# Sample blocks at alternate heads, a DMA rate of 280 in the list schedule, and later weights for the second head

## The chip, the cores and the metric

The kernel runs on 8 cores of one Trainium2 chip. Every core runs the same program on its own data; nothing is exchanged between cores. The metric is the device time of the slowest core in microseconds. A profile is one execution, read on the slowest of its cores (core 5 here). Names of the engines in profile rows: PE is TensorE (PEld its weight loads), DVE is VectorE, ACT is ScalarE, POOL is GpSimd, SP is SyncE, which only issues DMAs here.

## The reference

One inference step of a two-layer decoder, for 8 prompts of 2048 tokens and 128 samples of 4 new tokens, model width 1024. A core takes one prompt and 16 samples (64 sample tokens).

- Layer 0, HGRN2, 16 heads of 128 channels: `proj = x @ w_in` gives q, forget logit, value and gate for each head. With `f = lb + (1 - lb) * sigmoid(z)` the state is `S_t = diag(f_t) S_{t-1} + (1 - f_t) v_t^T` and the output `o_t = S_t^T q_t`; then a per-head RMS norm, times `silu(gate)`, `@ w_out`. A prompt starts from a zero state, a sample from its given state; both return their final states.
- Layer 1, chunked gMLP, chunks of 128 positions, 16 groups of 128 channels: u and v through gelu, v layer-normalised, `mixed = tril(W_s) v + b_s` in each group and chunk, `out = u * mixed * silu(z)`, `@ w_out`. The normalised v rows of the samples are an output.
- After each layer `x = LayerNorm(ALPHA * x + mixer(x))`.

## The kernel before, in words

**Tiling and stages.** A core works through its prompt in two passes of 1024 tokens (`sbi` 0 and 1), as 8 tiles of 128 tokens, or 2 blocks of 512 (`bi`). The 64 sample tokens are a ninth tile (`XTS`). A pass has these stages: transposed x in `XT`; layer 0's 16 heads, `for h in range(H)`, each with two prompt blocks (`l0_prompt`) and, for eight of the heads, one sample block (`l0_sample`); the output projection with layer norm (`outproj_ln`); layer 1's first eight groups of u and z (`uz`), the v tiles with the spatial gating (`v_tile`), the last eight groups of u and z, and the second output projection. Each head's sample block is computed once in the whole kernel, as its weights pass by: before, heads 0 to 7 in the first pass and heads 8 to 15 in the second (`if h // 8 == sbi`). The sample tile goes through the later stages in the second pass alone.

**A prompt block** (`l0_front`, `l0_prompt`, `l0_out`). TensorE makes four projections of the block (24 matmuls of 512 columns and 32 of 128 for the values). ScalarE makes tanh, two silu, a logarithm (L617) that needs the gate constants `lbc`, two exponentials, copies, and the norm's logarithm and exponential; functions of different tables need a table load between them. VectorE scans the logarithms (L640, L642), GpSimd scales the chunk states (L686) and multiplies by the gate (L706). A sample block does the same for 64 tokens, and in addition loads 2 x 512 KB of states on the SP queue, converts them to bf16 on ScalarE, multiplies values by a mask on VectorE (L731), adds into the states and stores 2 x 512 KB. Its state buffers `S0` exist twice, picked by `k = h % 2`.

**Weights.** The projection weights of head h lie in two of four `WH` buffers. `wia_load(h + 2)` stands behind head h: its two DMAs, issued by GpSimd, wait until head h's projections have read the buffers. They convert float32 to bf16 (512 KB land for 1 MB read). `wbig_load` brings an eighth of an output or v weight; in both passes the heads 1 to 8 each load one eighth of `woa`. At head 2 of the first pass the spatial weights are loaded too (`WST`, `WSM`, `GB`), at head 4 they are masked, 32 GpSimd products.

**Start.** `x_first(j)` loads an x tile as float32 into one of four staging buffers `XSF` (the same memory as `S0`), transposes it on TensorE, and copies it to `XT[j]` with ScalarE and VectorE. Before: tile 0, weights of head 0, tiles 1 to 3, sample tile, weights of head 1, tiles 4 to 7. The constants `lbc` come by two small DMAs of the SP queue (L533 and before) and some steps on VectorE and ScalarE (L534 to L540).

**The order of work.** No engine's order is written out by hand. The code records every operation with a cost and its dependences (`Plan.rec`, `Plan.dma`). `Plan.schedule` then plays the program through once: at each step it picks, among the ready operations of all engines, the one that can start first, and by priority where starts are within 0.05 us. The priority is the place in the program, less `early`, less the length of the chain behind the operation. The result is one fixed order for each engine. `Plan.emit` writes it out with semaphore waits. An engine does its list strictly in order; if an operation is late on the chip, all behind it on that engine wait. A DMA is an operation of the queue that issues it, and its landing is planned thus, with one pipe for all DMAs of the core:

```python
            if o.dma:
                dmafree = max(s + o.cost, dmafree) + o.nbytes / self.DMABW
                o.fin = dmafree + self.DMALAT
```

Before, `DMABW` is 200.0e3 bytes per us and `DMALAT` 2.0 us. `nbytes` is 1 << 20 for a weight DMA and 1 << 19 for a state DMA. The plan does not re-order anything on the chip, and it does not know what the chip really does.

Of the kernel before, what the change touches and what calls it, by code (L numbers as in the profile page):

```python
# [11 lines left out]
ALU = mybir.AluOpType  # L12
# [76 lines left out]
class Plan:  # L89
# [11 lines left out]
    DMABW = 200.0e3  # L101
# [227 lines left out]
def build_nc():  # L329
# [25 lines left out]
    lng = din("lng", [2, 1, 1024])  # L355
    lnb = din("lnb", [2, 1, 1024])
# [6 lines left out]
    with ExitStack() as es:  # L363
        S = Plan(nc, es)
# [50 lines left out]
        LNG = sb("LNG", [128, 1024], F32)  # L415
        LNB = sb("LNB", [128, 1024], F32)
# [85 lines left out]
        XSF = [S0[0][0], S0[0][1], S0[1][0], S0[1][1]]  # L502
# [40 lines left out]
        def lnload(l):  # L543
            S.dma("sp", LNG[:], lng[l, 0, :].partition_broadcast(128), LNG, True, 524288)
            S.dma("sp", LNB[:], lnb[l, 0, :].partition_broadcast(128), LNB, True, 524288)
# [35 lines left out]
        def wia_load(h):  # L581
            for hf in range(2):
                w = WH[(h % 2) * 2 + hf]
                S.dma("pool", w[:].rearrange("p (a b) -> p a b", b=512), wia[h, :, hf * 2048:(hf + 1) * 2048].rearrange("p (a b) -> p a b", b=512),
                      w, True, 1 << 20, early=300)
# [122 lines left out]
        def l0_sample(h):  # L708
            N = 64
            k = h % 2  # L710
# [114 lines left out]
        def v_tile(ti):  # L825
# [15 lines left out]
            for nb in range(4):  # L841
                V(lambda v, nb=nb: v.tensor_scalar(out=vg[nb][0:rows, :], in0=vg[nb][0:rows, :], scalar1=st[0:rows, 24:25], scalar2=st[0:rows, 26:27],  # L842
                                                   op0=ALU.subtract, op1=ALU.mult), (vg[nb], st), (vg[nb],), 0.4, port=True)
                P(lambda e, nb=nb: e.tensor_tensor(out=ng[nb][0:rows, :], in0=vg[nb][0:rows, :], in1=GB[0:rows, nb * 512:(nb + 1) * 512], op=ALU.mult),  # L844
                  (vg[nb], GB), (ng[nb],), 1.05)
# [37 lines left out]
        for sbi in range(2):  # L883
            if sbi == 0:
                x_first(0, 0, XSF[0])
                wia_load(0)
                for j in range(1, 4):
                    x_first(j, j * 128, XSF[j])
                x_first(8, 0, XSF[0])
                wia_load(1)  # L890
                for j in range(4, 8):
                    x_first(j, j * 128, XSF[(j + 1) % 4])
            else:
                lnload(0)
# [4 lines left out]
            for h in range(H):  # L899
# [8 lines left out]
                if h // 8 == sbi:  # L908
                    l0_sample(h)
# [22 lines left out]
                if sbi == 0 and h == 4:  # L932
# [24 lines left out]
                    lnload(0)  # L957
# [91 lines left out]
```

How the kernel before makes its waits and increments, by code:

```python
    def emit(self):  # L249
# [16 lines left out]
                key, val, sem, sval = tok[d]  # L266
                if kn.get(key, 0) >= val:
                    continue
                waits.append((sem, sval))
                for k, v in clock[d].items():
                    if kn.get(k, 0) < v:
                        kn[k] = v
            eng = self.eng[o.e]
            embed = not o.dma and o.e != "pe"
            for sem, sval in (waits[:-1] if embed else waits):
                eng.wait_ge(sem, sval)
            ins = None
            for n_, fn in enumerate(o.fns):
                ins = fn(eng)
                if n_ == 0 and embed and waits:
                    ins.wait_op(waits[-1][0], waits[-1][1], "sem-ge")
            if o.dma:
                b = o.sbuf
                if b.sem is None:
                    b.sem = self.newsem("d")
                b.cnt += 16
                ins.then_inc(b.sem, 16)
                tok[i] = (b, b.cnt, b.sem, b.cnt)
                if o.is_out:
                    outs.append(tok[i])
# [5 lines left out]
                sem = esem[o.e][-1]  # L296
                ins.then_inc(sem, 1)
                tok[i] = (o.e, q + 1, sem, q % self.EPOCH + 1)
            c = dict(kn)
            c[tok[i][0]] = tok[i][1]
            clock[i] = c
        fin = {}
        for key, val, sem, sval in outs:
            fin[key] = max(fin.get(key, (0, None)), (sval, sem), key=lambda t: t[0])
        for sval, sem in fin.values():
            self.eng["sp"].wait_ge(sem, sval)
```

## Time and profile before

| | before |
|---|---|
| median of 3 runs | 1448.02 us (1445.81 to 1459.31) |
| the profiled execution's own time | 1448.55 us |
| its span on core 5 | 1447.5 us |
| spans of the 8 cores | 1419.9 to 1447.5 us |
| TensorE busy | 1313.5 us (91%) |
| ScalarE busy | 918.5 us (63%) |
| VectorE busy | 901.2 us (62%) |
| GpSimd busy | 577.2 us (40%) |
| mean granted TensorE clock, core 5 | 0.959 |
| x tile load (ARENA<-xp), median from issue to landing | 3.5 us |

How to read it: the span runs from the first to the last instruction; the execution's own time has about 1 us around it. Busy shares are means over stages with different limits, so they do not say what a stage waits for. The first pass's heads run from about 22 to 430 us, the second's from about 745 to 1103 us; the rest are output projections and the gMLP layer.

### The profile page before, as it was taken

To read this page: it belongs to the slowest core of one execution; us is meant where nothing else is said; L and a number is where in the kernel's file an instruction comes from. 1 tells how busy PE (TensorE), PEld (TensorE's weight loads), DVE (VectorE), ACT (ScalarE), POOL (GpSimd) and SP (SyncE) were. 2 spreads that over 40 slices of the span, in tenths; PEclk is the share of its full clock that TensorE was granted. 3 is DMA by queue.
4 is the path that set the end of the run, shared out by engine and by line. 5 is a ranking of instruction groups with operands and counts; after the bars stand their busy time and mean duration, and the time that the engine had idled before them with its cause. 6 is when DMAs were issued, how large, how long until landed. Compare 5 with 4: busy or idle time off the path is not lost.

```text
span 1447.5 us, 25232 instructions; the slowest of 8 cores (1419.9 to 1447.5 us)
## 1 busy us (share of the span) xinstructions
PE 1313.5 (91%) x9592; PEld 710.2 (49%) x9592; DVE 901.2 (62%) x1932; ACT 918.5 (63%) x1543; POOL 577.2 (40%) x700
## 2 busy tenths in 40 slices
PE   6898887889979989997999999998988998999997
PEld 3555454545534434443455655555554443444443
DVE  1688775546757434752676666767786733476467
ACT  1899898879952434642149999999993244465310
POOL 3257554423330416563003444545463051677400
PEclk9999888889989999998999999999999999999999
DMA  8488585433322863097234556465544195319211
GB/s 197 124 151 156 129 160 104 92 55 59 60 59 73 108 97 59 11 159 121 74 102 90 92 92 93 91 148 150 119 122 126 58 130 88 60 30 132 44 54 70
DMA packets 61254, 142.58 MB, mean 98 GB/s; under 512 B 5584, under 2 KB 32208, under 8 KB 61136
## 3 DMA queue, kind: packets, MB, share of 16 engines
q0 software_dynamic: 41072, 78.80, 36.9%
q1 hardware_dynamic: 20064, 62.16, 13.9%
q8 instruction: 79, 1.29, 0.4%
q14 instruction: 39, 0.32, 0.1%
HBM read 192.73 MB, written 27.00 MB: 152 GB/s over the span
## 4 chain that ended last, share of the span: by engine, by line
PE 44%; ACT 31%; DVE 9%; DMA 9%; POOL 4%; issue 3%; SPq 0%; DVEq 0%; ACTq 0%; POOLq 0%
PE PS L326 43%; DMA WBIG<-wv 6%; ACT L617 3%; ACT ARENA L617 3%; ACT L612 3%; DMA WH<-wuz 2%; ACT PS L646 2%; DVE ARENA L640 2%; POOL ARENA L844 2%; ACT ARENA L612 2%; ACT ARENA L614 2%; ACT ARENA L702 2%; ACT ARENA L616 1%; ACT PS L650 1%; ACT ARENA L656 1%
## 5 line engine op out<-in xcount | busy, mean ns | idle before, releaser
L326 PE MATMUL PS<-XT,WH 128*128 128x512 bf16 x2560 | 600.3, 389 | 15.4 <-DMA WH<-wuz 10.5
L326 PEld LDWEIGHTS PS<-XT,WH 128*128 128x128 bf16 x2560 | 247.1, 100 | 306.9 <-issue 49.5
L326 PE MATMUL PS<-WBIG,OT 128*128 128x512 bf16 x1024 | 228.5, 383 | 4.0 <-POOL OT L706 3.3
L326 PEld LDWEIGHTS PS<-WBIG,OT 128*128 128x128 bf16 x1024 | 99.8, 99 | 123.5 <-issue 9.5
L326 PE MATMUL PS<-WBIG,XT 128*128 128x512 bf16 x512 | 119.5, 389 | 9.8 <-DMA WBIG<-wv 9.8
L326 PE MATMUL PS<-WH,XT 128*128 128x128 bf16 x2048 | 126.9, 221 | 0.7 <-DVE SCO L666 0.7
L326 PE MATMUL PS<-ARENA 128*128 128x128 bf16 (+4 forms) x1360 | 114.7, 214 | 12.3 <-DVE ARENA L651 3.8
L326 PEld LDWEIGHTS PS<-WH,XT 128*128 128x128 bf16 x2048 | 118.7, 99 | 6.1 <-issue 2.1
L706 POOL TENSOR_TENSOR OT<-ARENA 128x512 bf16<-128x512 f32 x64 | 81.2, 1270 | 96.8 <-DVE ARENA L704 96.8
L770 DVE BATCH_NORM_STATS2 ARENA<-ARENA 128x6 f32<-128x512 f32 (+1 forms) x136 | 93.8, 690 | 41.6 <-ACT ARENA L838 38.5
L813 DVE SCALAR_TENSOR_TENSOR ARENA<-ARENA,PS 128x512 f32<-128x512 f32 (+1 forms) x80 | 46.4, 592 | 108.7 <-ACT ARENA L812 108.7
L644 POOL TENSOR_TENSOR ARENA<-ARENA 128x5 f32<-128x5 f32 x64 | 17.6, 275 | 214.9 <-DVE ARENA L642 214.7
L640 DVE TENSOR_TENSOR_SCAN ARENA<-scm,ARENA 128x64 f32<-128x64 f32 x256 | 65.1, 314 | 58.1 <-ACT ARENA L617 57.6
L326 PEld LDWEIGHTS PS<-ARENA 128*128 128x128 bf16 (+2 forms) x1360 | 76.5, 103 | 42.6 <-issue 28.1
L844 POOL TENSOR_TENSOR ARENA<-ARENA,GB 128x512 bf16<-128x512 f32 (+1 forms) x68 | 83.2, 1245 | 32.6 <-DVE ARENA L842 32.4
L811 ACT ACTIVATE ARENA<-PS 128x512 f32<-128x512 f32 (+1 forms) x80 | 41.8, 523 | 85.6 <-PE PS L326 84.9
L773 ACT ACTIVATE ARENA<-ARENA,lbc 128x1 f32<-128x1 f32 (+1 forms) x51 | 15.0, 296 | 112.9 <-DVE ARENA L772 109.3
L326 PEld LDWEIGHTS PS<-WBIG,XT 128*128 128x128 bf16 x512 | 49.0, 100 | 73.9 <-issue 22.0
L686 POOL TENSOR_TENSOR ARENA<-ARENA 128x384 bf16<-128x384 f32 x64 | 61.4, 959 | 59.8 <-DVE ARENA L683 59.0
L812 ACT ACTIVATE ARENA<-PS 128x512 f32<-128x512 f32 (+1 forms) x80 | 41.8, 524 | 64.0 <-PE PS L326 63.9
L838 ACT ACTIVATE ARENA<-PS 128x512 f32<-128x512 f32 (+1 forms) x68 | 39.4, 597 | 65.4 <-PE PS L326 60.1
L625 DVE CAST ARENA<-PS 128x512 bf16<-128x512 f32 (+1 forms) x80 | 48.0, 602 | 44.7 <-PE PS L326 44.3
(162 smaller groups left out, 2250.2 us busy)
## 6 DMA issues: line engine op xcount, KB each, us to landing
WH<-wia POOLq DMA_DIRECT2D x64, 512.0 KB, 8.6
ARENA<-s SPq DMA_DIRECT2D x32, 512.0 KB, 5.9
sso<-ARENA SPq DMA_DIRECT2D x32, 512.0 KB, 4.3
WH<-wuz POOLq DMA_DIRECT2D x32, 512.0 KB, 9.0
ARENA<-xp SPq DMA_DIRECT2D x24, 512.0 KB, 3.5
WBIG<-woa POOLq DMA_DIRECT2D x16, 512.0 KB, 8.0
WBIG<-wv POOLq DMA_DIRECT2D x16, 512.0 KB, 26.4
WBIG<-wob POOLq DMA_DIRECT2D x16, 512.0 KB, 15.9
```

Of the source, the lines that this page charges most:

```text
L326: return lambda t: t.matmul(out(), lhsT=lhsT, rhs=rhs, start=start, stop=stop, skip_group_check=True)
L612: A(lambda a, b=b: a.activation(out=tz[:, 0:N], in_=b.v(N), func=AF.Tanh, scale=-0.5), (b,), (tz,), c_act(N), "tanh")
L617: A(lambda a: a.activation(out=lf[:, 0:N], in_=tz[:, 0:N], func=AF.Ln, scale=nc1, bias=c0), (tz, lbc), (lf,), c_act(N) + 0.2, "ln")
L625: V(lambda v, b=b: v.tensor_copy(out=Vt[0:rows, 0:ntile * 128], in_=b.v(ntile * 128, rows)), (b,), (Vt,), c_dve(ntile * 128))
L640: S.rec("dve", [lambda v, n=n: v.tensor_tensor_scan(out=Dm[:, n, 65:129], data0=scm[:, 1:65], data1=L3[:, n, 64:128], initial=0.0, op0=ALU ...
L686: P(lambda e: e.tensor_tensor(out=T3[:, n0:4, :], in0=Pst[:, n0:4, :], in1=G[:, n0:4].rearrange("p (c o) -> p c o", o=1).to_broadcast([128 ...
L706: P(lambda e: e.tensor_tensor(out=ot, in0=rs[:, 0:N], in1=tg[:, 0:N], op=ALU.mult), (rs, tg), otb, c_pool(N))
L770: V(lambda v, c=c, ap=ap: v.bn_stats(out=st[0:rows, c * 6:(c + 1) * 6], in_=ap), (pb,), (st,), 0.69)
L811: A(lambda a: a.activation(out=T2[:, 0:N], in_=bk[0].v(N), func=AF.Gelu_apprx_tanh), (bk[0],), (T2,), c_act(N), "gelu")
L812: A(lambda a: a.activation(out=T3[:, 0:N], in_=bk[1].v(N), func=AF.Tanh, scale=0.5), (bk[1],), (T3,), c_act(N), "tanh")
L813: V(lambda v: v.scalar_tensor_tensor(out=T3[:, 0:N], in0=T3[:, 0:N], scalar=1.0, in1=bk[1].v(N), op0=ALU.add, op1=ALU.mult), (T3, bk[1]), ...
L844: P(lambda e, nb=nb: e.tensor_tensor(out=ng[nb][0:rows, :], in0=vg[nb][0:rows, :], in1=GB[0:rows, nb * 512:(nb + 1) * 512], op=ALU.mult), ...
```

## The change

Six edits. (1) The planner's DMA rate goes from 200.0e3 to 280.0e3 bytes per us. (2) A head's sample block is done in the first pass if h is odd and in the second if h is even, and its state buffer is picked by `(h // 2) % 2`, so that the two buffers still alternate. (3) The planned cost of VectorE's subtraction in `v_tile` goes from 0.4 to 0.65 us. (4) At the start the weights of head 1 may be issued only after the last copy of x tile 3; then come tiles 4 to 7, each in the staging buffer `j % 4`, and the sample tile last. (5) `wia_load` and `lnload` can take an operation to wait for. (6) The first load of the layer-norm vectors (`LNG`, `LNB`), recorded at head 4 of the first pass, waits for that head's first prompt block.

```diff
-    DMABW = 200.0e3
+    DMABW = 280.0e3
...
-        def lnload(l):
-            S.dma("sp", LNG[:], lng[l, 0, :].partition_broadcast(128), LNG, True, 524288)
-            S.dma("sp", LNB[:], lnb[l, 0, :].partition_broadcast(128), LNB, True, 524288)
+        def lnload(l, after=None):
+            S.dma("sp", LNG[:], lng[l, 0, :].partition_broadcast(128), LNG, True, 524288, after=after)
+            S.dma("sp", LNB[:], lnb[l, 0, :].partition_broadcast(128), LNB, True, 524288, after=after)
...
-        def wia_load(h):
+        def wia_load(h, after=None):
             for hf in range(2):
                 w = WH[(h % 2) * 2 + hf]
                 S.dma("pool", w[:].rearrange("p (a b) -> p a b", b=512), wia[h, :, hf * 2048:(hf + 1) * 2048].rearrange("p (a b) -> p a b", b=512),
-                      w, True, 1 << 20, early=300)
+                      w, True, 1 << 20, early=300, after=after)
...
-            k = h % 2
+            k = (h // 2) % 2
...
-                                                   op0=ALU.subtract, op1=ALU.mult), (vg[nb], st), (vg[nb],), 0.4, port=True)
+                                                   op0=ALU.subtract, op1=ALU.mult), (vg[nb], st), (vg[nb],), 0.65, port=True)
...
                 for j in range(1, 4):
                     x_first(j, j * 128, XSF[j])
+                mark = len(S.ops) - 1
+                wia_load(1, after=mark)
+                for j in range(4, 8):
+                    x_first(j, j * 128, XSF[j % 4])
                 x_first(8, 0, XSF[0])
-                wia_load(1)
-                for j in range(4, 8):
-                    x_first(j, j * 128, XSF[(j + 1) % 4])
...
-                if h // 8 == sbi:
+                if h % 2 != sbi:
                     l0_sample(h)
...
-                    lnload(0)
+                    lnload(0, mark)
```

## Rows read from the trace of the kernel before

**Rows 1.** The page, part 4: the chain that ended last, shares by engine.

```profile
PE 44%; ACT 31%; DVE 9%; DMA 9%; POOL 4%; issue 3%; SPq 0%; DVEq 0%; ACTq 0%; POOLq 0%
```

**Rows 2.** Stretches: length, busy PE, PEld, DVE, ACT, POOL, granted clock, DMA share, GB/s.

```profile
56.00:237.00 181.00, 155.74 (x1456) 92.32 (x1456) 138.95 (x334) 167.20 (x286) 104.85 (x138) 0.92 0.74 143
237.00:317.00 80.00, 64.54 (x500) 37.26 (x501) 38.57 (x109) 61.12 (x92) 27.45 (x37) 0.81 0.40 75
...
762.00:913.00 151.00, 142.21 (x1343) 89.62 (x1344) 100.32 (x289) 142.88 (x217) 67.86 (x96) 1.00 0.54 87
```

**Rows 3.** Timeline of GpSimd, second pass: start us, duration, weight issues (behind heads 0, 6, 7, 13).

```profile
762.09 1.15 POOL L149 DMA_DIRECT2D WH<-wia  x2 [0.37 <-PE PS L326]
...
874.30 1.06 POOL L149 DMA_DIRECT2D WH<-wia  x2 [0.98 <-PE PS L326]
893.00 1.06 POOL L149 DMA_DIRECT2D WH<-wia  x2 [2.20 <-PE PS L326]
...
1038.33 1.14 POOL L149 DMA_DIRECT2D WH<-wia  x2 [1.71 <-PE PS L326]
```

**Rows 4.** The same, first pass: behind heads 0, 7, 8, 9 and 10.

```profile
56.02 1.13 POOL L149 DMA_DIRECT2D WH<-wia  x2 [0.29 <-issue]
...
233.32 1.13 POOL L149 DMA_DIRECT2D WH<-wia  x2 [0.52 <-PE PS L326]
...
262.98 1.13 POOL L149 DMA_DIRECT2D WH<-wia  x2 [1.09 <-PE PS L326]
286.87 1.12 POOL L149 DMA_DIRECT2D WH<-wia  x2
316.84 1.14 POOL L149 DMA_DIRECT2D WH<-wia  x2
```

**Rows 5.** Timeline of TensorE: first projections of heads 8, 9, 10; second pass, head 7.

```profile
243.13 3.62 PE L326 MATMUL PS<-XT,WH 128*128 128x512 bf16 x8
...
268.28 6.96 PE L326 MATMUL PS<-XT,WH 128*128 128x512 bf16 x24
...
297.34 7.78 PE L326 MATMUL PS<-XT,WH 128*128 128x512 bf16 x24
...
873.82 5.34 PE L326 MATMUL PS<-XT,WH 128*128 128x512 bf16 x24
```

**Rows 6.** Landing of the weights issued at 262.98; VectorE's scan of head 10.

```profile
DMA to landing us min/median/max: 8.4/9.4/10.3
...
306.19 0.84 DVE L640 TENSOR_TENSOR_SCAN ARENA<-scm,ARENA 128x64 f32<-128x64 f32 x4 [10.92 <-ACT ARENA L617]
```

**Rows 7.** Head 0's second and head 1's first weight load; transposes of x tile 3.

```profile
L149 POOL DMA_DIRECT2D WH<-wia x2: 538/538/539, 2.3 to 2.8; - x2
...
DMA to landing us min/median/max: 15.8/17.3/18.9
...
18.98 1.94 PE L554 MATMUL PS<-identF,ARENA 128*128 128x128 f32 x8 [3.38 <-DMA ARENA<-xp]
```

**Rows 8.** First projections; second `lbc` load with its landing; its use; first logarithm.

```profile
22.04 7.17 PE L326 MATMUL PS<-XT,WH 128*128 128x512 bf16 x24 [1.12 <-DVE XT L561]
...
21.97 0.33 SPq L149 DMA_DIRECT2D lbc<-lbl  x1
...
DMA to landing us min/median/max: 10.7/10.7/10.7
...
41.17 0.16 DVE L534 TENSOR_TENSOR lbc<-lbc 128x16 f32<-128x16 f32 x1
...
45.38 0.82 ACT L617 ACTIVATE ARENA<-ARENA,lbc 128x512 f32<-128x512 f32 x1
```

**Rows 9.** The eight `wv` loads of the first pass; the page's row of the v matmuls.

```profile
L149 POOL DMA_DIRECT2D WBIG<-wv x8: 745/770/834, 477.1 to 482.7; - x8
...
DMA to landing us min/median/max: 7.1/27.1/42.4
...
L326 PE MATMUL PS<-WBIG,XT 128*128 128x512 bf16 x512 | 119.5, 389 | 9.8 <-DMA WBIG<-wv 9.8
```

## The prediction

> **What bounds the kernel now.** First the page: TensorE is busy 91% of the span, but the chain of waits gives it only 44% and ScalarE 31% [rows 1]. Two regimes are mixed, so I read the stretches: the gMLP stages and output projections are TensorE's, the 16 recurrence heads of each pass are not. In the prompt-only heads of the second pass ScalarE works 142.88 of 151 us (95%), in the sample heads of the first 167.20 of 181 (92%) [rows 2]. These stretches go at ScalarE's pace, and a change of order can at best fill its gaps.
>
> Next, the pace of a head. GpSimd issues the weight loads of head h+2 when the projections of head h have read their buffer, so these issues mark the ends of heads. Second pass: 762.09 (head 0), 893.00 (head 7), 1038.33 (head 13) [rows 3]. So a prompt-only head takes 130.91/7 = 18.7 us and one with a sample block 145.33/6 = 24.2 us. First pass: 56.02 (head 0), 233.32 (head 7), 316.84 (head 10) [rows 4]. Its sample heads take 177.3/7 = 25.3 us, but heads 8 to 10, which have no sample block, take 83.5 us where 3 x 18.7 = 56.1 are due. **27.4 us are lost there.** Only in that stretch is ScalarE so far below its load elsewhere in mid-pass: 61.12 of 80 us (76%), the granted clock a mean 0.81 [rows 2].
>
> Where inside these heads? Head 7 ends at 233.32 and TensorE starts head 8's projections at 243.13; head 8 ends at 262.98, head 9's start at 268.28; head 9 ends at 286.87, head 10's start at 297.34 [rows 4, 5]: 9.8 + 5.3 + 10.5 = 25.6 us, nearly the whole loss. In the second pass a head's end is issued at 874.30 and the next projections have already begun at 873.82 [rows 3, 5]. What is awaited? No DMA: head 10's weights were issued at 263.0 and landed within 10.3 us, so they lay in SBUF 24 us before use [rows 5, 6]. The projections stand in TensorE's order behind the last small matmuls of the block before; with no projection, ScalarE has nothing, and VectorE's scan waits 10.92 us for the next logarithm [rows 6]. The orders of the engines are fixed at build time, by a list schedule whose single DMA pipe moves 200,000 bytes per us. I check that pipe with the code's sizes. A first-pass sample head moves two state loads and two stores (0.52 MB each), two projection weights and one output weight (1.05 MB each): 5.24 MB, 26.2 us at that rate, against 25.3 us of head. Head 2 adds WST, WSM and GB, 2.36 MB or 11.8 us, the later LNG 2.6; heads 1 to 7 add 0.9 each, 6.3. So some 21 us of pipe are planned to be outstanding when head 8 begins. A weight pair is issued one head (18.7 us) before use; its planned landing is 21 + 10.5 + 2 = 33 us off, so the scheduler starts the next head's projections up to 14 us late, and drains the block before meanwhile. A prompt-only head adds 3.15 MB or 15.7 us, so the queue lasts a few heads; heads 8 to 10 fit. In the second pass heads 0 to 7 need 15.7 of 18.7 us and heads 9 to 15 4.2 MB, 21 of 24.2: no queue, no gap.
>
> **The change part by part.** One profiled execution serves for all durations: span 1447.5 us, 1448.55 with what lies around it, 0.5 us above the median of 1448.02.
>
> (1) Rate 280,000 and sample blocks at alternate heads. Two heads now bring 5.24 + 3.15 = 8.39 MB, 30 us at the new rate, against 24.2 + 18.7 = 42.9 us of work; head 2's 2.36 MB and LNG are absorbed within a pair. The planned queue is gone, the gap with it. Below: zero, if the gap has another cause. Above: 27.4, the whole loss. The first holds the rest of sample block 7, of which 3 to 4 us must run somewhere. I take **-24**, near the row.
>
> (2) The even spreading itself. All 16 sample blocks remain, their ScalarE work remains, and both kinds of head are ScalarE's already, so I take **0**. Bounds: what sample heads differ by between the passes, 25.3 against 24.2 us [rows 3, 4], for 8 heads: 9 us either way.
>
> (3) The start. Head 1's weights are now issued after the fourth x tile's copy instead of at 3 us; x tiles 4 to 7 come before the sample tokens; the early LNB load goes to head 4, where its 5 us of DMA lie beside recurrence work (DMA share 0.74 there [rows 2]); late in the pass nothing reads it before about 430 us. Do the first x tiles gain? The fourth is there at 18.98 us, but head 0's own second half landed only at 2.3 + 15.8 = 18.1, head 1's first half at 2.8 + 18.9 = 21.7 [rows 7]. So an earlier tile is worth 0.9 us at most before head 0's weights are the last; I take 0.9, within the sum below.
> The Trainium skill has a rule that speaks against even that: "DMA: Bandwidth & Descriptors", section "Queues, rings and completion order", says that each DMA engine alternates between queue rows and takes one row's work in ring order. By it head 1's loads, behind head 0's in GpSimd's row, took nothing from SP's x tiles before 18.1: 0 instead of 0.9. The landings 18.1, then 21.7, agree with the order.
> The larger item is the gate constants (lbc). Their second load goes at 21.97, lands 10.7 us later at 32.7, and the VectorE step that uses it stands in the order behind work of sample block 0: it runs at 41.17, so the first logarithm of a head comes at 45.38 [rows 8]. Now LNB is not ahead of the load, sample block 0 is gone from the first head, and the faster planned pipe puts the step earlier; around 28 to 30 us is possible, 16 us sooner. But one prompt block costs TensorE some 9 us (7.17 us of projections and some 2 of values [rows 8]) and ScalarE as much, so TensorE's pace from 22 us caps what is won. Bounds 0 and -16; I take **-7**. Head 1's weights, issued at about 21 us and, by the loads of [rows 6, 7], 10 to 19 us on their way, are wanted at about 22 + 18 = 40 us: hidden; if not, up to 3 us. They wait on GpSimd, which has only small set-up work behind them.
>
> (4) Dependences moved by the placing. First pass: the last sample block is now head 15's, and the input buffers of the output projection overlap its S0B and VM, so these 3.5 us loads can no longer be made early. In the second pass this is so already, and an input tile is read only after the 16 matmuls of its first half: 0. The first state load after the pass change finds slot 0 free as before: 0. In return the second pass ends without a sample block.
>
> (5) The V stage. VectorE's subtraction is planned longer; TensorE is the bound there: 0. But the eighth load of wv lands 42.4 us after its issue at 482.7, 48 after the first one's at 477.1 [rows 9]; in the plan 8 x 1.05 MB now take 30 + 2, so TensorE's order may place V matmuls too early. Today it waits 9.8 us for wv in both passes together [rows 9]. Nothing else is ready before these landings, so the waits stay. Bounds: 0, and per pass the 16 us between 32 and 48 less the 5 waited today, +11. I take **+2** in all.
>
> Sum: -24 + 0 - 7 + 2 = -29; 1448.5 - 29 = 1419.5, **1420 us**.
>
> **The rivals.**
> A. The gap at heads 8 to 10 is not the planned queue but the slow clock: its mean is 0.81 there, 0.92 in the stretch before, where heads keep pace [rows 2]. But the 24 projections at 297.34 took 7.78 us against 5.34 at full clock [rows 5], 2.4 us more, and the gaps between the projections stay as long at any clock, so the clock looks like the gaps' result. Then only the start is won: 1448.5 - 7 = 1441.
> B. More is won: first-pass sample heads fall from 25.3 to 24.2 us (9 us), GpSimd's mask products of head 4 no longer meeting a sample head, and the earlier constants pay all 16 us instead of 7: 1420 - 18 = 1402.
> C. Slower: the plan runs ahead of the DMA. Place: the V stage and the loads after it, both passes. wv really takes 48 us; orders built on 30 leave TensorE waiting for WBIG up to 11 us more per pass, and in the head stretch nothing is won: 1448.5 - 7 + 22 = 1464. It ends on that side by over 1% from 11 us more per pass on, with heads 8 to 10 as slow as now. Against it: a head's weights land 8.4 and 10.3 us after their issue [rows 6]; the new rate plans 5.7 and 9.5 with an idle pipe.
> D. The change doesn't do what it says at the start (tiles not sooner, constants still late): 1420 + 7 = 1427, inside the forecast's range.
>
> **How the numbers follow.** The forecast with D 0.68, A 0.13, B 0.11, C 0.08. The main case spreads over 1403 to 1440 by its bounds; with B's 1402 and A's 1441 the range 1397 to 1443 leaves out C and the tails. One per cent is 14.5 us, about what a measurement of this kernel tells from no change. Faster by more (under 1433.5): most of the main case, 0.56, B, 0.10 = 0.66. Same: A, 0.12, the main case's upper end, 0.11, a little of C = 0.25. Slower: 0.09.
>
> **What would show it.** (1) Issues of head weights in the first pass 42 to 44 us apart by pairs, none over 27 us, the clock not near 0.81 in any 80 us, no gap over 3 us between one head's last projection and the next one's first, and head 10's end some 30 us earlier. (2) Sample heads of the first pass at 24 to 25 us. (3) First projection at 20 to 22 us, first logarithm at 28 to 35. (5) Waits for WBIG<-wv about 5 us per pass. The prediction is wrong if three consecutive first-pass heads without new work still take 25 us or more, or if waits for wv exceed 15 us.

## The result and the profile after

**Time.** The changed kernel has a median of 1437.66 us (12 runs) beside 1445.96 us for the kernel before (12 runs). The ratio is 0.9932 [0.9903, 0.9961]: 10 us or 0.7% faster, where 28 us were forecast. A second measurement of the changed kernel (e0_after below) gave 0.9885 [0.9808, 0.9961]. All ratios and timed means of cores here leave out executions in which one die ran slower than the other; the medians are over all executions.

First the page of the changed kernel: span, chain of waits, and TensorE's two groups that wait for weights of the gMLP layer (the last columns: idle time before the group, and what ended most of it).

```profile
span 1427.3 us, 25233 instructions; the slowest of 8 cores (1397.5 to 1427.3 us)
...
PE 50%; ACT 26%; DVE 12%; DMA 7%; POOL 3%; issue 3%; SPq 0%; DVEq 0%; POOLq 0%; ACTq 0%
...
L326 PE MATMUL PS<-XT,WH 128*128 128x512 bf16 x2560 | 605.2, 390 | 18.0 <-DMA WH<-wuz 13.0
...
L326 PE MATMUL PS<-WBIG,XT 128*128 128x512 bf16 x512 | 117.3, 383 | 8.2 <-DMA WBIG<-wv 8.2
```

The profiled execution took 1428.42 us, 20 less than the one of before, although the medians differ by 8. ScalarE's part of the chain has fallen from 31% to 26% [rows 1]. The view of the cores explains part of the disagreement:

```profile
core 3: 1427.3 us, clock 0.966
...
core 7: 1397.5 us, clock 0.982
```

The spans of one execution lie 30 us apart at granted clocks of 0.966 and 0.982, and the slowest core sets the time. The mean of the 8 spans is steadier. In the timed executions it fell from 1433.2 to 1418.1 us, that is 15 us (in e0_after's measurement from 1434.2 to 1414.0, 20 us); in the two profiles it falls from 1437.6 to 1412.8, since before was caught 4.4 above its usual mean and after 5.3 below its own. So below I compare stages by the mean over the 8 cores, and hold the sum against the timed means.

The first two stretches of [rows 2], in the changed kernel (length, busy PE, PEld, DVE, ACT, POOL, granted clock, DMA share, GB/s):

```profile
56.00:237.00 181.00, 164.82 (x1498) 100.79 (x1497) 132.57 (x335) 164.15 (x272) 98.22 (x140) 0.92 0.68 127
237.00:317.00 80.00, 73.55 (x707) 45.16 (x706) 61.84 (x160) 75.95 (x127) 38.95 (x47) 1.00 0.49 105
```

The stretch in which ScalarE worked 61.12 of 80 us at a clock of 0.81 now has 75.95 of 80 at 1.00. The same stretch holds other heads now; over the changed kernel's heads 8 to 10 (204.77 to 269.99) the clock is 0.97, where it was 0.82 over those of before. GpSimd's timeline shows the heads. Its weight issues behind heads 0, 7, 8, 9, 10 and 13 of the first pass, then behind heads 0 and 13 of the second:

```profile
42.63 1.08 POOL L149 DMA_DIRECT2D WH<-wia  x2 [9.36 <-PE PS L326]
...
204.77 1.15 POOL L149 DMA_DIRECT2D WH<-wia  x2 [2.31 <-PE PS L326]
226.15 1.15 POOL L149 DMA_DIRECT2D WH<-wia  x2 [1.37 <-PE PS L326]
248.43 1.14 POOL L149 DMA_DIRECT2D WH<-wia  x2
269.99 1.14 POOL L149 DMA_DIRECT2D WH<-wia  x2 [3.01 <-PE PS L326]
...
332.94 1.14 POOL L149 DMA_DIRECT2D WH<-wia  x2
...
739.69 1.14 POOL L149 DMA_DIRECT2D WH<-wia  x2 [5.11 <-PE PS L326]
...
1024.96 1.15 POOL L149 DMA_DIRECT2D WH<-wia  x2 [1.35 <-PE PS L326]
```

Heads 8 to 10 take 269.99 - 204.77 = 65.2 us instead of 83.5 [rows 4], and one of them now carries a sample block (due: 18.7 + 24.2 + 18.7 = 61.6). TensorE's timeline at the border of heads 7 and 8, and of 8 and 9 (answering to [rows 5]):

```profile
203.61 0.61 PE L326 MATMUL PS<-WH,XTS 128*64 128x128 bf16 x8
204.31 1.89 PE L326 MATMUL PS<-XT,WH 128*128 128x512 bf16 x8
...
223.65 1.95 PE L326 MATMUL PS<-WH,XT 128*128 128x128 bf16 x32
...
226.87 1.46 PE L326 MATMUL PS<-XT,WH 128*128 128x512 bf16 x6
```

Head 8's projections start 0.5 us before head 7's end is issued, head 9's 0.7 us after head 8's. The borders of 9.8, 5.3 and 10.5 us are gone.

**Stages.** Each core's TensorE timeline gives the borders: first projection, first output-projection matmul, first V matmul, and so on. Durations in us, mean of 8 cores of each profile; "V + u/z" is the V stage and the eight groups of u and z after it, both passes; "end" is the last matmul. The timed columns are the median, the ratio to the kernel before and the mean over the cores in timed executions.

The borders are not equally clean in all kernels, since the planner may mix work of two stages. In the kernel before, eight projections of the second pass stand ahead of the last 16 matmuls of the first pass's output projection:

```profile
743.76 1.89 PE L326 MATMUL PS<-XT,WH 128*128 128x512 bf16 x8
745.49 3.62 PE L326 MATMUL PS<-WBIG,OT 128*128 128x512 bf16 x16
```

Its 341.6 us for the second heads (likewise e8_start's and e9_v065's) count from behind these matmuls; from the first projection they are 346.9. In the changed kernel the last matmuls of head 15 of the first pass run inside the output projection. So two columns go over such borders: P1 is the first pass's heads with the output projection behind them, P2 the second pass's heads with the output projections before and behind them. Where the columns disagree, P1 and P2 decide.

| kernel | heads, pass 1 | P1 | heads, pass 2 | P2 | V + u/z | end | median | ratio [95%] | core mean |
|---|---|---|---|---|---|---|---|---|---|
| before | 398.4 | 460.0 | 341.6 | 474.2 | 347.5 | 1428.3 | 1446 | 1 | 1433.2 |
| after | 361.3 | 426.6 | 345.8 | 479.5 | 352.1 | 1403.5 | 1437.7 | 0.9932 [0.9903, 0.9961] | 1418.1 |
| e0_after | 360.4 | 425.7 | 346.0 | 479.6 | 349.3 | 1400.0 | 1437.2 | 0.9885 [0.9808, 0.9961] | 1414.0 |
| e1_rate | 376.8 | 438.7 | 351.5 | 479.9 | 352.5 | 1417.0 | 1443.4 | 0.9959 [0.9926, 0.9991] | 1426.9 |
| e2_spread | 383.9 | 445.7 | 338.6 | 472.9 | 346.8 | 1411.2 | 1437.7 | 0.9882 [0.9818, 0.9945] | 1418.9 |
| e3_after_200 | 374.3 | 438.9 | 338.0 | 472.5 | 342.0 | 1398.9 | 1427.3 | 0.9839 [0.9777, 0.9901] | 1411.9 |
| e5_rate_spread | 375.7 | 437.9 | 345.6 | 479.3 | 362.9 | 1426.2 | 1448.1 | 0.9996 [0.9964, 1.0027] | 1433.2 |
| e6_v04 | 360.0 | 425.4 | 345.3 | 479.1 | 357.5 | 1407.7 | 1440.1 | 0.9946 [0.9908, 0.9983] | 1420.4 |
| e7_rate_first | 361.2 | 426.2 | 338.6 | 472.7 | 346.1 | 1390.4 | 1412.0 | 0.9747 [0.9681, 0.9812] | 1399.6 |
| e8_start | 404.3 | 466.3 | 340.9 | 473.6 | 345.2 | 1430.8 | 1450.3 | 1.0029 [0.9999, 1.006] | 1437.6 |
| e9_v065 | 398.2 | 459.7 | 341.0 | 473.6 | 342.2 | 1421.3 | 1447.3 | 0.9999 [0.9966, 1.0032] | 1432.8 |
| e10_wia_half | 376.6 | 438.3 | 351.3 | 477.9 | 344.2 | 1406.4 | 1435.0 | 0.9892 [0.9865, 0.9918] | 1415.9 |
| e11_rest_175 | 367.5 | 432.1 |  | 495.6 | 355.1 | 1428.2 | 1451.9 | 1.0015 [0.9988, 1.0041] | 1436.1 |
| e12_heads_280 | 360.4 | 425.5 | 344.1 | 477.8 | 348.0 | 1396.5 | 1421.7 | 0.9813 [0.9754, 0.9871] | 1403.6 |

From before to after: first projection -1.0, P1 -33.4, V + u/z +4.6, P2 +5.3; the first eight groups of u and z and the last output projection keep their length. At the last matmul that is 1403.5 - 1428.3 = -24.8, rounding aside. The first pass's heads and their output projection gave more than was forecast for the whole kernel. What comes behind them gave nearly 10 us back.

### The profile page after: what moved, and what is told of

Read it like the earlier page. It is cut to its first block, busy times and chain, and to the rows that moved or that the text cites. A ratio compares the mean times of both kernels' runs of the same rounds, so it can differ in the third digit from the quotient of the medians.

```text
span 1427.3 us, 25233 instructions; the slowest of 8 cores (1397.5 to 1427.3 us)
## 1 busy us (share of the span) xinstructions
PE 1309.1 (92%) x9592; PEld 707.3 (50%) x9592; DVE 911.1 (64%) x1932; ACT 900.5 (63%) x1531; POOL 582.6 (41%) x700
## 4 chain that ended last, share of the span: by engine, by line
PE 50%; ACT 26%; DVE 12%; DMA 7%; POOL 3%; issue 3%; SPq 0%; DVEq 0%; POOLq 0%; ACTq 0%
PE PS L326 49%; DMA WH<-wuz 6%; DVE ARENA L640 3%; ACT L617 2%; ACT ARENA L617 2%; ACT L612 2%; ACT PS L646 2%; ACT ARENA L612 2%; ACT ARENA L702 2%; ACT ARENA L614 1%; ACT PS L650 1%; ACT ARENA L616 1%; ACT ARENA L699 1%; DVE ARENA L642 1%; ACT L616 1%
## 5 line engine op out<-in xcount | busy, mean ns | idle before, releaser
L640 DVE TENSOR_TENSOR_SCAN ARENA<-scm,ARENA 128x64 f32<-128x64 f32 x256 | 76.8, 360 | 32.5 <-ACT ARENA L617 32.0
L686 POOL TENSOR_TENSOR ARENA<-ARENA 128x384 bf16<-128x384 f32 x64 | 67.0, 1047 | 63.2 <-DVE ARENA L683 63.0
L326 PEld LDWEIGHTS PS<-WBIG,XT 128*128 128x128 bf16 x512 | 48.3, 98 | 69.6 <-issue 15.7
L647 DVE SCALAR_TENSOR_TENSOR ARENA<-ARENA,PS 128x512 bf16<-128x512 f32 x64 | 43.7, 682 | 41.7 <-ACT PS L646 41.3
```

Source lines behind the costliest of these rows:

```text
L326: return lambda t: t.matmul(out(), lhsT=lhsT, rhs=rhs, start=start, stop=stop, skip_group_check=True)
L640: S.rec("dve", [lambda v, n=n: v.tensor_tensor_scan(out=Dm[:, n, 65:129], data0=scm[:, 1:65], data1=L3[:, n, 64:128], initial=0.0, op0=ALU ...
L647: V(lambda v: v.scalar_tensor_tensor(out=Bb[:], in0=tz[:], scalar=1.0, in1=e2.v(), op0=ALU.add, op1=ALU.mult), (tz, e2), (Bb,), c_dve(512))
L686: P(lambda e: e.tensor_tensor(out=T3[:, n0:4, :], in0=Pst[:, n0:4, :], in1=G[:, n0:4].rearrange("p (c o) -> p c o", o=1).to_broadcast([128 ...
```

## The experiments

Two theories stood against each other. **Plan:** the order is worse where the planner's DMA pipe is out of step with the loads, and the gaps at heads 8 to 10 were its queue. **Work:** the gaps came from the load of the heads themselves (sample blocks, slow clock), and spreading closes them whatever the rate.

**e0_after**: the changed kernel once more, no edit.

> The changed kernel once more, beside the others on one chip: a measure of how far the stage table of one profile scatters. Median 1430 to 1440 us. Mean over the cores of first-pass heads 358 to 365 us, second-pass heads 343 to 349, v and u/z stages together 347 to 357.

Ratio 0.9885; the stages repeat within 1 us except V + u/z (2.8). It is one repetition only. A difference of 4 us and more in a stage is read below as one, a smaller one is not.

**e1_rate**: before with the new rate alone. **e2_spread**: before with the alternate heads alone. **e5_rate_spread**: both (old start, cost 0.4).

```diff
# e1_rate, e5_rate_spread
-    DMABW = 200.0e3
+    DMABW = 280.0e3
# e2_spread, e5_rate_spread
-            k = h % 2
+            k = (h // 2) % 2
...
-                if h // 8 == sbi:
+                if h % 2 != sbi:
```

> Only the planner's DMA rate is changed, 200 to 280 thousand bytes per us; sample blocks, start and V cost as before. Theory P (the planned DMA queue opens the gaps before heads 8, 9 and 10 of the first pass): first-pass heads, from the first projection to the first output projection, fall from 398 us by 20 to 28, to 370 to 378; no gap over 3 us at a head border. Rival S (the even spreading does it): heads stay at 393 to 403. Rival C (the plan runs ahead of the DMA): the waits for wv and wuz grow by over 5 us each. Whole kernel by P: 10 to 20 us under before (ratio 0.986 to 0.993).

> Only the sample blocks move to alternate heads (and their buffer index with them); rate 200, start as before. Theory P: with 200 two heads bring 8.39 MB, 42 us of planned pipe against 43 of work, so the queue planned by the start and by WST, WSM, GB at head 2 never empties and only spreads out: half of the gap loss stays, first-pass heads 380 to 392 us. Rival S: 361 to 370. Second pass's heads: P and S 338 to 346 us (before 341.6). Whole kernel 0 to 10 us under before.

> Rate 280 and alternate heads, without the new start, without the V cost and the later LNG and LNB. It tells what the start edits are worth: first-pass heads 361 us if the start is worth nothing, 368 if it is worth the 7 us forecast for it. First logarithm near 45 us if only the order of the loads moves it, near 35 if the rate does. Whole kernel 0.986 to 0.994 of before.

The rate alone, with all sample blocks in the old heads, takes 21.6 us off the first heads. GpSimd's weight issues of e1_rate behind heads 7 to 10 (before: 233.32 to 316.84, [rows 4]):

```profile
241.59 1.15 POOL L149 DMA_DIRECT2D WH<-wia  x2 [0.75 <-PE PS L326]
...
265.95 1.12 POOL L149 DMA_DIRECT2D WH<-wia  x2 [1.45 <-PE PS L326]
...
284.26 1.12 POOL L149 DMA_DIRECT2D WH<-wia  x2 [0.21 <-issue]
...
303.00 1.14 POOL L149 DMA_DIRECT2D WH<-wia  x2
```

Heads 8 to 10, with the same work as before, take 303.00 - 241.59 = 61.4 us instead of 83.5. Spreading alone takes 14.5 off the first heads, both together 22.7: they close the same gap and do not add. But the kernels at 280 lose behind the first heads: e1_rate 5.7 us in P2 and 5.0 in V + u/z against before, e5_rate_spread 5.1 and 15.4, which puts it back at before's time. Only e2_spread, at the old rate, loses nothing there. Both kernels at 280 came out slower than expected (0.9959 where 0.986 to 0.993 was said, 0.9996 where it was 0.986 to 0.994): the ranges given for them had no room for this loss.

**e3_after_200**: the changed kernel at the old rate.

```diff
-    DMABW = 280.0e3
+    DMABW = 200.0e3
```

> The changed kernel with the planner's rate back at 200; all other edits stay. Theory P: the rate is needed for most of the first pass's gain; first-pass heads 378 to 390 us (changed kernel 361, before 398). Rival S: 361 to 368. Theory G (the faster rate costs in the gMLP stages and output projections: from head end to kernel end it loses as TensorE's order runs ahead of the landings): without it the V stages and the u/z groups behind them come back to before's 106.3 + 67.1 and 113.3 + 60.8 us, from 108.7 + 66.2 and 110.3 + 66.9. Whole kernel within 8 us of before.

It loses 13.0 us in the first heads, gains 7.8 in the second and 10.1 in V + u/z against the changed kernel, and at 0.9839 [0.9777, 0.9901] is no slower than it (0.9932 and 0.9885). It was expected within 8 us of before; its timed mean of the cores is 21 us below. The new rate, over the whole program, pays nothing once the sample blocks are spread.

**e6_v04**: the changed kernel with the V stage's cost back. **e9_v065**: before with that cost alone (its diff is this one reversed).

```diff
-                                                   op0=ALU.subtract, op1=ALU.mult), (vg[nb], st), (vg[nb],), 0.65, port=True)
+                                                   op0=ALU.subtract, op1=ALU.mult), (vg[nb], st), (vg[nb],), 0.4, port=True)
```

> The changed kernel with the planned cost of VectorE's subtraction back at 0.4. Heads unchanged in both passes (361, 346). Theory V (the truer cost gives the v stages a better order): the two v stages together 225 to 229 us instead of 219, whole kernel 5 to 10 us over the changed kernel. Forecast's own view (TensorE is the bound there, the cost is worth nothing): 217 to 221, same time.

> Before with the planned cost of VectorE's subtraction at 0.65 alone. Theory V: the two v stages together 210 to 214 us instead of 219.6, all else as before, ratio 0.994 to 0.998. Forecast's own view: 218 to 221, ratio 1.000.

In the profiles the longer cost takes 5.3 us off V + u/z in before (347.5 to 342.2: the V stages alone -11.0, the u/z after them +5.7) and 5.4 in the changed kernel (357.5 to 352.1). In time neither shows: 0.9999 for e9_v065, and 0.9946 beside 0.9932. A small effect of the size seen is possible, none is shown. e6_v04's 357.5 is 5 to 8 us above the two profiles of the changed kernel (352.1 and 349.3).

**e8_start**: before with the start alone (edits 4 to 6).

```diff
-                x_first(8, 0, XSF[0])
-                wia_load(1)
+                mark = len(S.ops) - 1
+                wia_load(1, after=mark)
...
-                    x_first(j, j * 128, XSF[(j + 1) % 4])
+                    x_first(j, j * 128, XSF[j % 4])
+                x_first(8, 0, XSF[0])
...
-                    lnload(0)
+                    lnload(0, mark)
```

> Before with the start edits alone: head 1's weights after x tile 3, sample tile last, LNB at head 4. Rate 200, sample blocks at heads 0 to 7 and 8 to 15. First projection 21 to 22 us. By the forecast's term 7 us, by the difference of 14 between the changed kernel and the one with rate and spreading alone up to 14: first-pass heads 384 to 391 us, gaps at heads 8 to 10 still there (their three intervals sum to over 75). If the start pays only with a sample-free head 0: 394 to 400. Whole kernel 0.990 to 0.996.

Alone the start does not pay: first heads +5.9, ratio 1.0029, where 0.990 to 0.996 was expected. In the spread kernels it does: e5_rate_spread to e6_v04, which differ by these edits, 375.7 to 360.0. Part of that is the border: over column P1 it is 437.9 to 425.4, that is -12.5, and the timed mean of the cores falls by 12.8. At the old rate, e2_spread to e3_after_200 (which also has edit 3), P1 falls by 6.8 and the timed mean by 7.0. That the start needs a first head without a sample block is likely, but spreading changes all other heads too, so it was not shown.

The start edits were to bring the first logarithm forward. ScalarE's first logarithm in e1_rate and e5_rate_spread (rate 280, old start), then in e8_start and e3_after_200 (rate 200, new start):

```profile
42.22 1.14 ACT L617 ACTIVATE ARENA<-ARENA,lbc 128x512 f32<-128x512 f32 x2
40.82 0.81 ACT L617 ACTIVATE ARENA<-ARENA,lbc 128x512 f32<-128x512 f32 x1
...
45.28 1.51 ACT L617 ACTIVATE ARENA<-ARENA,lbc 128x512 f32<-128x512 f32 x2
46.32 1.51 ACT L617 ACTIVATE ARENA<-ARENA,lbc 128x512 f32<-128x512 f32 x2
```

The second `lbc` load landed 10.4 us after its issue in the first two and 3.9 and 4.8 us after it in the last two. So the planned rate moves the logarithm, and the earlier landing does not.

**e7_rate_first**: the changed kernel, with 280 only for operations recorded before the first pass's output projection and 200 for all later ones. It tests the reading that the new rate helps in the first heads and costs behind them.

```diff
-            tail[o.i] = (o.cost + (2.0 + o.nbytes / self.DMABW if o.dma else 0.0)) + max([tail[u] for u in o.users], default=0.0)
+            tail[o.i] = (o.cost + (2.0 + o.nbytes / (self.DMABW if o.i < self.split else 200.0e3) if o.dma else 0.0)) + max([tail[u] for u in o.users], default=0.0)
...
-                dmafree = max(s + o.cost, dmafree) + o.nbytes / self.DMABW
+                dmafree = max(s + o.cost, dmafree) + o.nbytes / (self.DMABW if o.i < self.split else 200.0e3)
...
+            if sbi == 0:
+                S.split = len(S.ops)
```

> The changed kernel, but the planner uses 280 only for operations recorded before the first pass's output projection and 200 for all later ones. Theory R (the rate pays in the first pass's heads and costs behind them): first-pass heads as in the changed kernel, 358 to 364 us; second-pass heads 336 to 341 instead of 345.8; the two v stages together 207 to 212 instead of 219. Whole kernel 1408 to 1420 us, ratio 0.974 to 0.982, better than the changed kernel by 14 to 25 and than the changed kernel at 200 by 5 to 12. Rival N (the differences between these orders are luck of the draw and not the rate's): second-pass heads and v stages scatter as before, ratio 0.985 to 0.995.

It keeps the first heads (361.2), has the second heads of e3_after_200 (338.6) and 346.1 for V + u/z; end -13.1 us against the changed kernel. Timed: 1412 us, ratio 0.9747 [0.9681, 0.9812]; the changed kernel has 0.9932 [0.9903, 0.9961] and, measured again, 0.9885 [0.9808, 0.9961]. **This version is faster than the kernel before and than the changed kernel** (its interval just touches that of the second measurement; against e3_after_200 the intervals overlap). It is 2.5% or 36 us faster than before: with the rate kept to the stretch that had the queue, the change gives what was forecast and more. Its waits of TensorE for the gMLP weights (total us, times, longest; the changed kernel has 8.2 for wv and 13.0 for wuz):

```profile
PE PS L326 <- DMA WH<-wuz: 8.7, 1, 8.7
PE PS L326 <- DMA WBIG<-wv: 8.4, 2, 4.5
```

**e12_heads_280**: e7_rate_first, but with 280 in the second pass's heads too.

```diff
-                dmafree = max(s + o.cost, dmafree) + o.nbytes / (self.DMABW if o.i < self.split else 200.0e3)
+                dmafree = max(s + o.cost, dmafree) + o.nbytes / (self.DMABW if o.i < self.split or self.lo <= o.i < self.hi else 200.0e3)
...
+            S.lo = len(S.ops)
...
+            else:
+                S.hi = len(S.ops)
```

(`lo` and `hi` are set ahead of and behind the heads of each pass; the line of the chain lengths is changed in the same way.)

> The rate is 280 in the heads of both passes and 200 in output projections and gMLP. If the rate itself makes the order of the second pass's heads worse, they take 344 to 348 us as in the changed kernel, whole kernel 1416 to 1424. If their loss came only from the state in which the stages before leave the plan, they take 336 to 341, whole kernel 1408 to 1415. V and u/z stages together 343 to 348 us in both.

Second heads 344.1 (+5.5 against e7_rate_first; P2 +5.1), V + u/z 348.0 (+1.9), end +6.1; ratio 0.9813 [0.9754, 0.9871], between the two, with intervals that overlap both. By the stages nearly half of the 13 us is lost in the second pass's heads and not in the stages that load wv.

**e10_wia_half**: the opposite handle. Before, at the old rate, with the head weights alone counted as half their bytes (they are written as bf16, 512 KB).

```diff
-                      w, True, 1 << 20, early=300)
+                      w, True, 1 << 19, early=300)
```

> Before, with one number changed: the planner counts a head's weight load as 0.52 MB instead of 1.05; the loads themselves, the rate 200, the placing and the start are as before. Theory P (a planned DMA queue opens the gaps): a sample head is 4.19 MB, 21 us of planned pipe, the queue empties before head 8, and heads 8 to 10 of the first pass sum to 56 to 64 us instead of 83.5; first-pass heads 370 to 382 us. Rival (the rate works through all planned times, not through this queue): heads 8 to 10 over 75, first-pass heads 390 to 402. Stages behind the first pass's heads like before's (v stages together 215 to 222), so the whole kernel 0.983 to 0.993.

Behind heads 7 to 10, from its timeline of GpSimd:

```profile
238.95 1.14 POOL L149 DMA_DIRECT2D WH<-wia  x2 [1.47 <-PE PS L326]
...
260.74 1.14 POOL L149 DMA_DIRECT2D WH<-wia  x2 [0.23 <-issue]
...
278.96 1.12 POOL L149 DMA_DIRECT2D WH<-wia  x2 [0.21 <-issue]
...
297.70 1.15 POOL L149 DMA_DIRECT2D WH<-wia  x2
```

Heads 8 to 10 take 297.70 - 238.95 = 58.8 us; 56.1 were due, 83.5 it was. One number of the planner, no work moved, no rate changed: the planned queue opened the gaps. It too loses in the second pass (P2 +3.7), but nothing in V + u/z (344.2; its wv and wuz are planned as before).

**The plan's own times** say the same. `schedule` computes a start for each operation and a landing for each load, and this can be worked through without the chip. For the kernel before, it lands the weights of heads 8, 9 and 10 at 237.3, 260.9 and 287.1 us, and puts their first projections at 237.8, 260.9 and 287.3: as soon as they land. For e1_rate it lands them at 200.5, 223.6 and 245.5 and puts the projections at 212.8, 234.1 and 252.9: none of the three waits for its landing any more. The rate, and `nbytes` too, enter the plan twice, in the pipe and in the length of the chain that sets an operation's priority, and each edit here changed both. With 280 in the pipe alone the plan is like e1_rate's (211.5, 233.2, 252.0), with 280 in the chain lengths alone like before's (238.8, 264.7, 288.3). So it is the pipe, by the plan; no run on the chip separates the two.

**e11_rest_175**: e7_rate_first with 175 in place of 200 for what is recorded later. The expectation took this as a truer rate that does no harm. It had not added up the pipe: two of the heads 1 to 8 of the second pass bring 8.39 MB, 47.9 us at that rate, more than their 42.9 us of work.

```diff
-                dmafree = max(s + o.cost, dmafree) + o.nbytes / (self.DMABW if o.i < self.split else 200.0e3)
+                dmafree = max(s + o.cost, dmafree) + o.nbytes / (self.DMABW if o.i < self.split else 175.0e3)
```

(The line of the chain lengths is changed in the same way.)

> As the kernel with 280 for the first pass's heads, but 175 instead of 200 for all later operations, which is what wv's eight loads really make (8.4 MB in 48 us). If the loss behind the heads comes from planning landings too early, more truth does no harm: v and u/z stages together 338 to 346 us (346.1 with 200, 352.1 in the changed kernel), second-pass heads 335 to 341, whole kernel 1405 to 1414. If the differences are accidents of an order, it may come out anywhere from 1405 to 1435.

Weight issues behind heads 5 to 8 of the second pass:

```profile
847.81 1.10 POOL L149 DMA_DIRECT2D WH<-wia  x2 [1.15 <-PE PS L326]
...
874.45 1.13 POOL L149 DMA_DIRECT2D WH<-wia  x2
...
901.69 1.13 POOL L149 DMA_DIRECT2D WH<-wia  x2
...
928.08 1.13 POOL L149 DMA_DIRECT2D WH<-wia  x2 [1.39 <-PE PS L326]
```

26.6, 27.2 and 26.4 us a head, with and without a sample block alike, where e7_rate_first takes 42.0 for heads 6 and 7 together (issues at 838.29 and 880.32). TensorE begins the next projections 5.2 and 6.2 us after the first two of these issues:

```profile
853.01 3.11 PE L326 MATMUL PS<-XT,WH 128*128 128x512 bf16 x7 [0.17 <-issue]
...
880.66 3.19 PE L326 MATMUL PS<-XT,WH 128*128 128x512 bf16 x7 [0.22 <-issue]
```

From head 0's row to head 13's it needs 310.4 us against 281.5, and the ratio is 1.0015: the whole gain of e7_rate_first is gone. Both outcomes that were expected on record, 1405 to 1414 and 1405 to 1435, were missed. Of the 37.8 us lost at the last matmul against e7_rate_first, 22.9 lie in P2, 9.0 in V + u/z, and 5.9 in P1, where the planned landings have the same rate as in e7_rate_first and only the chain lengths behind them have changed. The border of its second heads is mixed as in the kernel before, so that cell is left empty.

## Why the prediction was right and wrong

**What bounds the kernel, and term (1), -24: right, mechanism and size.** The gap at heads 8 to 10 was the planned queue. Three edits that touch only the plan show it: e1_rate (-21.6 in the first heads), e10_wia_half (-21.8), and e11_rest_175 in reverse. Rate and spreading together, e5_rate_spread, gave -22.7. The prediction's sum for the queue has one slip: it lets every prompt-only head add 3.15 MB, but the output weights come only behind heads 1 to 8, so heads 9 and 10 add 2.1 MB, 10.5 us each. That empties the queue within three heads and fits rows 4, where the gap is at heads 8 to 10 and head 11 takes 17.4 us again. **Rival A fell** with it: the clock is 1.00 in the same stretch once the projections come without gaps, and came back without any change aimed at it.

**Term (2), 0 for spreading: wrong in a detail.** At the old rate spreading alone is worth -14.5 in the first heads, since it thins the same planned queue; beside the new rate it adds 1.1. As a term of this sum 0 was near.

**Term (3), -7 for the start: right in sign, but its mechanism failed.** e5_rate_spread to e6_v04 gives -15.7 in the first heads and -12.5 over P1; at the old rate it is -9.6 and -6.8. So the size of 7 was met at the old rate, but not for the stated reason, which was luck. The timeline of the changed kernel, SyncE, VectorE and ScalarE:

```profile
20.20 0.38 SPq L149 DMA_DIRECT2D lbc<-lbl  x1
...
35.01 0.16 DVE L534 TENSOR_TENSOR lbc<-lbc 128x16 f32<-128x16 f32 x1
...
42.02 1.52 ACT L617 ACTIVATE ARENA<-ARENA,lbc 128x512 f32<-128x512 f32 x2
```

The load landed 4.5 us after its issue, at 24.7 instead of 32.7 [rows 8], but the step that uses it still stands behind other work and runs at 35.01. The first logarithm came at 42.02; 28 to 35 was forecast, 45.38 it was. And these 3.4 us belong to the rate and not to the load: in five kernels at 200, with either start, the logarithm comes at 45.1 to 46.3 (before, e2_spread, e3_after_200, e8_start, e10_wia_half), in e1_rate and e5_rate_spread at 42.2 and 40.8 with the late load. From e5_rate_spread to e6_v04 it even comes 1.2 us later. The gain came elsewhere. Between these two, head 0's weight issue moves from 50.73 to 42.59, head 1's not at all (66.08, 66.31), and head 13's from 344.19 to 332.05, in small steps of which the largest is head 2 (32.0 to 26.8 us). So the order of later heads improved with the start; which of edits 4 to 6 does that was not separated. In the kernel before, the same edits made some first-pass heads worse (e8_start, head 5: 39.4 us, before 32.6).

The x tiles were worth about what was bounded: the first projection started at 20.83 instead of 22.04, 1.0 us sooner on the mean of the cores, released by the last tile's copy. Head 0's second half of weights, in GpSimd's queue ahead of head 1's, landed 15.2 us after its issue with head 1's loads moved away, 16.1 in e8_start, 15.8 with them in place [rows 7]. By the rule of the Trainium skill, "DMA: Bandwidth & Descriptors", section "Queues, rings and completion order", which the prediction weighed, loads behind it in its row's ring order cost it nothing, and the trace agrees by these three landings. Whether they cost SP's tiles the 1.0 us, against that rule, or whether LNB's load did, which moved too, no run here tells.

**Term (4), 0: not tested by itself.** The output projections behind the heads took 3.7 us more in the first pass and 3.3 in the second, but work of head 15 crosses those borders in the profiles of the spread kernels, so these figures are no loss of the output projections by themselves. They are contained in P1 and P2.

**Term (5), +2 for the V stage, and nothing at all for the second pass's heads: this is the step that failed.** The prediction priced the new rate only where a planned queue had to go. Behind the first pass's heads there was no queue to remove, and there the rate had only costs: in the changed kernel 6.8 us in P2 (479.5 against 472.7 in e7_rate_first) and 6.0 in V + u/z (352.1 against 346.1; 3.2 by e0_after's profile). One edit takes both back, 13.1 us at the last matmul, and in time 0.9932 or 0.9885 becomes 0.9747, that is 20 to 27 us, about as much as the forecast had been too high. Rival C had the direction, "the plan runs ahead of the DMA", and the condition wrong: it needed no head stretch without gain, and its price was not paid at wv. TensorE's waits for wv were 8.2 us against 9.8 before [rows 9], 5.7 in e0_after. Those for wuz were 13.0 and 9.5 against 10.5, no clear change, but without the longer V cost (e6_v04) they are

```profile
PE PS L326 <- DMA WH<-wuz: 22.5, 3, 9.0
```

against 1.0 for wv; e1_rate and e5_rate_spread, at 280 too and without that cost, have 16.0 and 18.4. The kernels that plan the gMLP stages at 200, and e11_rest_175 at 175, have 5.6 to 10.5. So it is the weights after the V stage that come late, not those of it. The zero for VectorE's planned cost was wrong in the profiles by some 5 us and is not shown wrong in time.

**Why the second heads suffer stays open in its mechanism.** All kernels in which head weights are planned fast there lose 4 to 7 us in P2: e1_rate 5.7 and e10_wia_half 3.7 against before, e5_rate_spread 6.4 against e2_spread, e12_heads_280 5.1 and the changed kernel 6.8 against e7_rate_first. The place is not the same in all: e1_rate and e10_wia_half lose it behind head 13's issue (60.3 and 59.5 us to the output projection, before 52.6) and nothing from head 0's to head 13's (274.8 and 276.6, before 276.1); the changed kernel loses 3.3 us up to there and 3.5 behind. No DMA is awaited in these heads. TensorE's largest waits in the second heads, changed kernel, then e7_rate_first:

```profile
PE PS L326 <- DVE ARENA L647: 10.0, 12, 1.5
PE PS L326 <- ACT ARENA L699: 5.0, 8, 1.3
```

```profile
PE PS L326 <- DVE ARENA L647: 6.8, 11, 1.4
PE PS L326 <- ACT ARENA L699: 4.1, 7, 1.4
```

Those are many short waits inside the blocks, 4 us more in these two rows. That the next head's projections are then put ahead of small matmuls that ScalarE or VectorE needs is the natural reading, but it was only argued.

**The total.** Forecast -29; stages -24.8 in one profile against one. That closeness is partly luck: the heads and their output projection (P1) with the first projection gave -34 where -31 was forecast, what comes behind took nearly 10 back where +2 was forecast, and the two profiles were 4.4 above and 5.3 below their kernels' usual mean. Timed, the mean of the cores fell by 15 us and the slowest core's time by 10 (20 and 17 in the second measurement), because the cores of the changed kernel lie further apart: an execution's time is 17 and 15 us above the mean of its cores, in the three sets of the kernel before 15, 12 and 12. The spread goes with the granted clock; why the cores of one execution get different clocks no run here tells.

Of the signs to look for: pairs of head ends were 42.0 to 43.8 us apart from head 7 on, as said; one head of 27.5 us was over the 27; head 10's end came 46.9 us earlier instead of some 30, because three of the sample blocks before it had moved to later heads (3 x 5.5 us), which the forecast forgot.

## What to carry to other kernels

A constant of a static planner, like its DMA rate, is not right or wrong for a kernel but for a stretch: price a new value in every stage that loads something, the ones that ran well above all, and set it where its queue shows. Before a profiled difference of one execution is believed on 8 cores, compare the mean over the cores in profile and timed runs; here that separated 15 us from 25. Add up a planner's pipe for every stretch before its rate is touched: 175 for 200, meant to be truer, brought a queue and gaps of 5 to 6 us back. And look at the plan's own times: a gap that the planner put there stands in them.

## What was not expected of the hardware

Cores that run the same program on equal shapes differed by 30 us of span in one execution, at granted clocks of 0.966 to 0.982, and a reordering alone changed by how much: over the timed executions the slowest and the fastest core lie 35 and 32 us apart in the changed kernel (two measurements), 22 to 27 in the kernel before (three), 25 in e7_rate_first. And the clock did follow the order: 0.81 in 80 us with gaps of 5 to 10 us between projections, 1.00 in the same 80 us without them.
